# A hybrid encoder block on one core: another bank for a few columns, sixteen blocks in the first selection, splits two ahead, and a last norm per tile

## The chip, the cores and the metric

The kernel runs on one core of a Trainium2 chip. Its metric is the device time of one execution in microseconds (us), the median of several runs. Five engines work side by side and meet only at semaphores: PE (TensorE, matmuls), DVE (VectorE), ACT (ScalarE), POOL (GpSimd) and SP (SyncE, which here only issues DMAs). All tensors come from and go to HBM.

## The reference

512 tokens and 16 meta tokens of width 1024 pass one layer. Cut to what matters here:

```python
h = layer_norm(concat([meta, x]))                       # embed
y = hybrid_mixer(h)        # retention (4 heads) and gated DeltaNet (8 heads), merged, times w_out
h = layer_norm(ALPHA * h + y)
q = (h @ w_q).reshape(L, 8, 2, 128)                      # expert retrieval, 8 heads
s = einsum('lhpd,hpnd->lhpn', q, sub_keys)               # 128 keys on each of two sides
# top 16 of each side, top 16 of the 256 sums -> 16 of 128 * 128 experts per head and token
y = sum over the 8 * 16 chosen of  gelu(h . u[expert]) * gate * v[expert]
out = layer_norm(ALPHA * h + y)[:, 16:]                  # ALPHA = 2 ** 0.25
```

## The kernel before, in words

All large matmuls take float32 operands split in two bfloat16 halves, high and low, and multiply three pairs of halves (`pair_matmul`, L149). ACT makes the high half (a copy), POOL the low half (value minus high half). Both are queued per 128x1024 slice, and PE waits for the low one.

**Retention** (0 to about 460 us) loops over 4 heads. Per head PE projects q, k, v and a gate, scores, outputs, and turns the normalised rows (`turn_rows`, L480). Every product has a PSUM bank in the list `order`; `wait_free` before a product waits until the bank's last reader is done. The 16 meta columns of the keys (`km`) are produced together with k0 and k1, so the wait for their bank stands in front of k0 (bank 2). In a head k0 follows right behind the turned rows y0 to y3 (banks 3 to 6) of the head before it, whose last readers are the low halves that DVE makes (L625). k1 is in bank 3.

**Retrieval** (`retrieve`, about 1415 to 1840 us). The 512 tokens are four tiles. DVE runs the top-k selection of a tile (`tile`), a serial chain of about 80 us. Beside it PE works through the first expert layer for the 384 tokens of tiles 0 to 2 (`Hidden`), in 128 blocks of 128 experts: per block n, SP loads 512 KB of u; ACT splits it (`split_hi`, L1805), POOL makes the low half (`split_lo`, L1821), PE runs 24 matmuls (`form`, L149 with 384 columns), ACT applies gelu (`apply_gelu`, L1813) and SP stores the result. `us` has two slots, so the split of block n+2 waits until block n is formed. `SHARES` says how many blocks run beside each tile's selection: 12, 20, 20, 20. ACT's Exp of the selection stands four blocks before the end of a share and waits for DVE. At the end of a share PE turns the chosen columns, ACT copies them (`picked`, L2025), and PE computes the next tile's scores (L1977).

For the last tile (128 tokens, the first that is selected) the dot products are done row by row instead: POOL gathers u rows for one of the 128 picks k (`gather`, L1874, 512 KB each, by indirect DMA), DVE multiplies and sums them with the tile's rows (`dot`, L1883). A gather waits until the dot that last used its slot is done (4 slots, in `spread` 6).

**Spread** (`spread`, about 1840 to 2160 us) does the other 56 blocks. In the first 48, the busy ones, it also scatters the gates of 4 tokens at a time into dense 128x128 grids: DVE makes one-hot tiles (L2234, L2238), ACT scaled low parts (`low_halves`, L2277), PE 16 small matmuls per block (L2264) behind the block's `form`, ACT copies the result (L2288), and stores 512 KB chunks during four of the six spans of 8 blocks. DVE does 3 dots per two blocks, each in front of the next one-hot tile. The order on ACT per block is split of n+1, gelu of n, two copies, eight low parts; on POOL it is low half of n, then one or two gathers. The last 8 blocks are plain (form, gelu, split). 8 dots are left for them. SP stores blocks 124 to 127 and loads the first four blocks of the next stage; behind the store of block 124 it waits for all 128 dots, since the value slots served as gather slots. The other three stores are queued behind that wait.

**Experts** (`experts`, about 2160 to 2703 us) is the second layer: per block 18 matmuls (L2443) that accumulate in banks 0 to 5 from the first block (`start=first`) to the last; DVE multiplies the gates in (L2487, L2490), makes the low half of the product (L2492), and adds one gathered row of v to the last tile's sum, which is in banks 6 and 7 (`own`, L2497). At the end DVE adds ALPHA times h (L2507).

**Finish** (`finish`, about 2704 us to the end) normalises all four tiles in step: statistics on DVE (L2558), Sqrt on ACT, shift and scale on ACT (L2543), gain on DVE (L2571), bias on POOL (L2550), and the stores.

Each stage is a `Block`; all engines meet at its end.

## Time and profile before

| what | value |
|---|---|
| median of 3 runs | 2732.01 us (2730.4 to 2733.27) |
| profiled execution, its own time | 2730.7 us |
| its span, first to last instruction | 2728.9 us |
| mean granted TensorE clock | 0.968 of full speed |
| busy: PE, DVE, ACT, POOL | 2471.7, 1637.2, 998.7, 1214.1 us |
| last matmul begins | 2701.94 us |
| first and last part of the finish | 2704.71 to 2728.9 us |

Start times are microseconds from the span's start. "Idle before" an instruction is how long its engine had nothing to run, with what ended that wait. The granted clock is the share of 2.4 GHz that TensorE was allowed.

### The profile page before, as it was taken

The numbers are of one execution on the slowest core, as the hardware profiler recorded it, in microseconds if no ns is written. First come the engines' busy times: TensorE is split into PE (matmuls) and PEld (weight loads), VectorE is DVE, ScalarE is ACT, GpSimd is POOL, SyncE is SP. The second block draws the span as 40 slices with busy tenths as digits, with TensorE's granted clock in tenths as the row PEclk, the third lists the DMA queues.
The fourth block names the chain that finished last, engine by engine and source line by source line (L and its number), as shares of the span: only waits on it lengthen the run. The fifth ranks groups of instructions, "written<-read, shape, count | busy, mean of one in ns | idle before, by whom it ended". The sixth has DMA issues, their size and how long they took to land. (4 is left out here: it accounts for less than half of the span.)

```text
span 2728.9 us, 43142 instructions
## 1 busy us (share of the span) xinstructions
PE 2471.7 (91%) x14285; PEld 1389.3 (51%) x14285; DVE 1637.2 (60%) x3379; ACT 998.7 (37%) x1740; POOL 1214.1 (44%) x744
## 2 busy tenths in 40 slices
PE   5999998987999999988979899987888899999995
PEld 3444443444777777775434555555555444444442
DVE  5023132026777777763340878888888477777877
ACT  4212212213333333332312333337888333333332
POOL 4312303313121222211513466666666677777775
PEclk9999998998999999989989999999999999999998
DMA  5302202120000100001322387777998899999995
GB/s 186 100 20 72 88 5 93 62 81 32 31 23 31 31 31 31 8 0 62 108 74 96 117 271 246 244 255 251 375 340 327 266 330 327 329 329 328 329 327 197
DMA packets 174309, 440.24 MB, mean 161 GB/s; under 512 B 17409, under 2 KB 83585, under 8 KB 174097
## 3 DMA queue, kind: packets, MB, share of 16 engines
q1 hardware_dynamic: 132752, 288.20, 30.6%
q0 software_dynamic: 36864, 134.23, 14.8%
q10 hardware_dynamic: 4608, 16.78, 1.6%
q8 instruction: 41, 0.67, 0.1%
q14 instruction: 44, 0.35, 0.0%
HBM read 395.11 MB, written 44.04 MB: 161 GB/s over the span
## 5 line engine op out<-in xcount | busy, mean ns | idle before, releaser
L149 PE MATMUL bank<-hT_hi,hid_u_hi 128*128 128x384 bf16 x1024 | 337.0, 329 | 67.2 <-POOL hid_u_lo L1821 41.2
L1821 POOL TENSOR_TENSOR hid_u_lo<-hid_u,hid_u_hi 128x1024 bf16<-128x1024 f32 x128 | 291.6, 2278 | 213.1 <-ACT hid_u_hi L1805 212.5
L149 PE MATMUL bank<-hT_lo,hid_u_hi 128*128 128x384 bf16 x1024 | 336.9, 329 | 0.0
L149 PE MATMUL bank<-hT_hi,hid_u_lo 128*128 128x384 bf16 x1024 | 336.5, 329 | 0.0
L204 POOL TENSOR_TENSOR ret_w_lo<-ret_w_raw,ret_w_hi 128x1024 bf16<-128x1024 f32 x72 | 153.3, 2162 | 393.6 <-ACT ret_w_hi L199 393.6
L2477 POOL TENSOR_TENSOR ex_v_lo<-ex_v,ex_v_hi 128x1024 bf16<-128x1024 f32 x128 | 272.3, 2127 | 121.0 <-ACT ex_v_hi L2460 120.9
L2443 PE MATMUL bank<-ex_v_hi,ex_gated_hi 128*128 128x512 bf16 x768 | 291.4, 379 | 27.7 <-DVE ex_gated_lo L2492 9.4
L2443 PE MATMUL bank<-ex_v_hi,ex_gated_lo 128*128 128x512 bf16 x768 | 291.6, 380 | 0.0
L2443 PE MATMUL bank<-ex_v_lo,ex_gated_hi 128*128 128x512 bf16 x768 | 291.6, 380 | 0.0
L2463 ACT ACTIVATE ex_gated_hi<-ex_gated 128x384 bf16<-128x384 f32 x128 | 66.9, 523 | 349.5 <-DVE ex_gated L2490 311.4
L2497 DVE SCALAR_TENSOR_TENSOR wide<-ex_row,row_gated,wide 128x1024 f32<-128x1024 f32 x128 | 164.9, 1288 | 49.0 <-DMA ex_row<-in_peer_v,row_index 47.3
L149 PEld LDWEIGHTS bank<-hT_hi,hid_u_hi 128*128 128x128 bf16 x1024 | 100.6, 98 | 154.3 <-issue 86.8
L1319 POOL TENSOR_TENSOR dn_q_decayed<-dn_exp_b,dn_q_k 128x512 f32<-128x512 f32 x16 | 19.9, 1266 | 323.1 <-DVE dn_q_k L1356 323.1
L2487 DVE TENSOR_TENSOR ex_gated<-ex_gated,ex_weights 128x256 f32<-128x256 f32 x128 | 163.2, 1275 | 0.0
L1813 ACT ACTIVATE hid_gelu<-bank 128x384 f32<-128x384 f32 x128 | 62.7, 490 | 258.3 <-PE bank L149 254.4
L2443 PEld LDWEIGHTS bank<-ex_v_hi,ex_gated_hi 128*128 128x128 bf16 x768 | 74.8, 97 | 161.6 <-issue 43.5
L2472 POOL DMA_INDIRECT ex_row<-in_peer_v,row_index x128 | 123.2, 963 | 28.5 <-DVE wide L2501 9.8
L149 PEld LDWEIGHTS bank<-hT_hi,hid_u_lo 128*128 128x128 bf16 x1024 | 100.9, 99 | 68.0 <-issue 2.4
L2460 ACT ACTIVATE ex_v_hi<-ex_v 128x1024 bf16<-128x1024 f32 x128 | 133.2, 1041 | 3.4 <-PEq L2189 3.4
L1805 ACT ACTIVATE hid_u_hi<-hid_u 128x1024 bf16<-128x1024 f32 x128 | 134.2, 1048 | 0.2 <-ACT ex_grid L2288 0.2
L149 PEld LDWEIGHTS bank<-hT_lo,hid_u_hi 128*128 128x128 bf16 x1024 | 100.8, 98 | 60.1 <-issue 2.2
L204 POOL TENSOR_TENSOR dn_w_lo<-dn_w_raw,dn_w_hi 128x1024 bf16<-128x1024 f32 x36 | 78.7, 2198 | 107.6 <-ACT dn_w_hi L199 107.6
(485 smaller groups left out, 5720.3 us busy)
## 6 DMA issues: line engine op xcount, KB each, us to landing
hid_u<-in_peer_u SPq DMA_DIRECT2D x128, 512.0 KB
ex_v<-in_peer_v SPq DMA_DIRECT2D x128, 512.0 KB, 5.4
ret_w_raw<-in_w_ret SPq DMA_DIRECT2D x60, 512.0 KB, 4.3
expert_hidden<-hid_gelu SPq DMA_DIRECT2D x128, 192.0 KB
ex_gated<-expert_hidden SPq DMA_DIRECT2D x128, 192.0 KB
dn_w_raw<-in_w_dn SPq DMA_DIRECT2D x36, 512.0 KB, 3.6
expert_weights<-ex_grid ACTq DMA_DIRECT2D x32, 512.0 KB
ex_weights<-expert_weights SPq DMA_DIRECT2D x64, 256.0 KB
```

Source lines behind the costliest of these rows:

```text
L149: last = nc.tensor.matmul(out, left[l], right[r], start=start and i == 0, stop=stop and i == len(PASSES) - 1)
L204: self.nc.gpsimd.tensor_tensor(self.pairs[slot][1][:, m % 4, :, :], self.raw[:, m % self.RING, :, :], self.pairs[slot][0][:, m % 4, :, :], ...
L1805: self.nc.scalar.activation(self.us[0][:, m % 2, :, :], self.u32[:, m % RING, :, :], ACT.Copy).then_inc(self.u_hi, 1)
L1813: self.nc.scalar.activation(self.act_out[:, m % RING, :], self.core.banks[4 + m % 2][:, 0:DENSE], ACT.Gelu).then_inc(self.gelu, 1)
L1821: self.nc.gpsimd.tensor_tensor(self.us[1][:, m % 2, :, :], self.u32[:, m % RING, :, :], self.us[0][:, m % 2, :, :], ALU.subtract).then_inc ...
L2443: last = nc.tensor.matmul(core.banks[u][:, :], gs[l][:, slot, t * P:(t + 1) * P], vs[r][:, slot, half * 512:(half + 1) * 512], start=first ...
L2460: nc.scalar.activation(vs[0][:, m % SLOTS, :], v32[:, m % RING, :], ACT.Copy)\
L2463: nc.scalar.activation(gs[0][:, m % SLOTS, :], g32[:, m % RING, :], ACT.Copy)\
L2472: nc.gpsimd.indirect_dma_start(row[:, n % RING, :], None, rows_dram[:, :], bass.IndirectOffsetOnAxis(ap=incoming.index[:, n:n + 1], axis=0))\
L2477: nc.gpsimd.tensor_tensor(vs[1][:, n % SLOTS, :], v32[:, n % RING, :], vs[0][:, n % SLOTS, :], ALU.subtract).then_inc(s["v_lo"], 1)
L2487: nc.vector.tensor_tensor(out_part, out_part, wt[:, m % RING // 2, :, m % 2, :], ALU.mult)
L2497: nc.vector.scalar_tensor_tensor(out=own[:, :], in0=row[:, m % RING, :], scalar=incoming.row_gated[:, cols], in1=own[:, :], op0=ALU.mult, ...
```

## The change

Four edits. (1) `km` goes to bank 7 and `v2` to bank 4. (2) The first share has 16 blocks, so retrieval does 76 and the spread stage 52, with 4 plain ones. (3) ACT splits block n+2 right behind gelu of block n; POOL's low halves are one more block ahead, so blocks 76 and 77 are split before and at the start of the spread stage; in the spread stage a block's gathers are queued in front of the low half of n+2. (4) PE starts the sums of the last stage with ALPHA times h (a float32 matmul with a scaled identity), DVE normalises straight from PSUM, tile by tile, the gathered tile first, with gain and bias folded into two operations; `finish` is gone as a stage, ACT only takes the roots and POOL has no part.

```diff
@@ -377,8 +377,8 @@
         act_steps, dve_steps, logit_ready, strip_arg, strip_ready, q_ready, k_ready, var_ready, std_ready, y_ready = (
             core.sem("ret_" + n) for n in ("act_steps", "dve_steps", "logit_ready", "strip_arg", "strip_ready",
                                            "q_ready", "k_ready", "var_ready", "std_ready", "y_ready"))
-        order = ([("q0", 0), ("q1", 1), ("k0", 2), ("k1", 3), ("km", 4)]
-                 + [("v0", 5), ("v1", 6), ("v2", 7), ("v3", 0), ("v4", 1)]
+        order = ([("q0", 0), ("q1", 1), ("k0", 2), ("k1", 3), ("km", 7)]
+                 + [("v0", 5), ("v1", 6), ("v2", 4), ("v3", 0), ("v4", 1)]
                  + [("g0", 2), ("g1", 3), ("g2", 4), ("g3", 5)]
                  + [("s0", 6), ("s1", 7), ("s2", 0), ("s3", 1), ("s4", 2)]
                  + [("o0", 3), ("o1", 4), ("o2", 5), ("o3", 6)]
@@ -1722,7 +1722,7 @@
 RING = 4
 DENSE = SEQ - P
 TILES = (NT - 1,) + tuple(range(NT - 1))
-SHARES = (12, 20, 20, 20)
+SHARES = (16, 20, 20, 20)
 PICKS = PH * TOPK
 BESIDE_TILE = 16
 BESIDE_TURN = 3
@@ -2002,11 +2002,12 @@
                             g = 4 * (n + weights.blocks) + c
                             weights.hi(act, g, g, n % weights.blocks)
                 hidden.split_hi(act, 0, 0)
+                hidden.split_hi(act, 1, 1)
                 gathered.hold_x(act)
                 def step(n, m):
-                    hidden.split_hi(act, n + 1, m + 1)
                     hidden.apply_gelu(act, n, m)
+                    hidden.split_hi(act, n + 2, m + 2)
                 for t in range(NT):
                     for c in range(4):
@@ -2039,6 +2040,7 @@
                                 k < min((s - 1) * BESIDE_TILE + j + 1 + AHEAD, (NT - 1) * BESIDE_TILE):
                             gathered.gather(pool, k)
                             k += 1
+                hidden.split_lo(pool, blocks, blocks)
             @block.vector
             def _(dve):
@@ -2280,8 +2282,8 @@
                 def step(n, m, side, turn, in_span, u0):
-                    hidden.split_hi(act, n + 1, m + 1)
                     hidden.apply_gelu(act, n, m)
+                    hidden.split_hi(act, n + 2, m + 2)
                     for u in range(u0, u0 + per):
                         bk.wait_full(act, f"w{u}", turn)
                         token = in_span * TURN + u * G
@@ -2328,9 +2330,9 @@
                     span_steps(spans - 2 + side, side, False, side == 0)
                 def plain(n, m):
-                    if n < BLOCKS - 1:
-                        hidden.split_hi(act, n + 1, m + 1)
                     hidden.apply_gelu(act, n, m)
+                    if n < BLOCKS - 2:
+                        hidden.split_hi(act, n + 2, m + 2)
                 for n in range(blocks + busy, BLOCKS):
                     plain(n, RING + n % RING)
@@ -2338,15 +2340,20 @@
             @block.gpsimd
             def _(pool):
+                hidden.split_lo(pool, blocks + 1, blocks + 1)
                 for k in range(dots_before, dots_before + RING):
                     gathered.gather(pool, k, dots_before)
                 k = dots_before + RING
                 for n in range(blocks, BLOCKS):
-                    hidden.split_lo(pool, n, n)
                     for _ in range((1, 2)[n % 2] if n < blocks + busy else 1):
                         if k < PICKS:
                             gathered.gather(pool, k, dots_before)
                             k += 1
+                    if n + 2 < BLOCKS:
+                        hidden.split_lo(pool, n + 2, n + 2)
+                while k < PICKS:
+                    gathered.gather(pool, k, dots_before)
+                    k += 1
                 assert k == PICKS
@@ -2386,11 +2393,12 @@
             .then_inc(self.arrived["weights"][slot], 16)
-def experts(core, incoming, acc):
+def experts(core, incoming, a, acc, out, ident):
...
-        names = "v_hi v_lo gated gated_hi gated_lo used row_added summed".split()
+        gain = sbuf(nc, ctx, "fin_gain", [P, D])
+        bias = sbuf(nc, ctx, "fin_bias", [P, D])
+        stats = sbuf(nc, ctx, "fin_stats", [P, NT, 12])
+        mv = sbuf(nc, ctx, "fin_mv", [P, NT, 2])
+        rstd = sbuf(nc, ctx, "fin_rstd", [P, NT])
+        scaled_ident = sbuf(nc, ctx, "ex_scaled_ident", [P, P])
+        names = ("v_hi v_lo gated gated_hi gated_lo used row_added summed ident_ready gb_in fin_steps var_ready std_ready "
+                 "row_ready stored").split()
         s = {n: core.sem("ex_" + n) for n in names}
...
                 over_blocks(sp, RING, BLOCKS, load)
+                sp.dma_start(gain[:, :], a["ln2_g"].partition_broadcast(P)).then_inc(s["gb_in"], 16)
+                sp.dma_start(bias[:, :], a["ln2_b"].partition_broadcast(P)).then_inc(s["gb_in"], 16)
+                for turn, tile in enumerate(ORDER):
+                    sp.wait_ge(s["row_ready"], turn + 1)
+                    sp.dma_start(out[tile * P:(tile + 1) * P, :], acc[:, tile, :]).then_inc(s["stored"], 16)
+                sp.wait_ge(s["stored"], 16 * NT)
...
-                                                    start=first and i == 0, stop=last_one and i == 2)
+                                                    start=False, stop=last_one and i == 2)
...
+                pe.wait_ge(s["ident_ready"], 1)
+                for u, (half, t) in enumerate(UNITS):
+                    nc.tensor.matmul(core.banks[u][:, :], scaled_ident[:, :], acc[:, t, half * 512:(half + 1) * 512],
+                                     start=True, stop=False)
...
+                for turn in range(NT):
+                    act.wait_ge(s["var_ready"], turn + 1)
+                    nc.scalar.activation(rstd[:, turn:turn + 1], mv[:, turn, 1:2], ACT.Sqrt)\
+                        .then_inc(s["std_ready"], 1)
...
+                nc.vector.tensor_scalar(scaled_ident[:, :], ident[:, :], ALPHA, None, ALU.mult)\
+                    .then_inc(s["ident_ready"], 1)
-                for u, (half, t) in enumerate(UNITS):
-                    dve.wait_ge(s["summed"], u + 1)
-                    part = acc[:, t, half * 512:(half + 1) * 512]
-                    nc.vector.scalar_tensor_tensor(out=part, in0=part, scalar=ALPHA, in1=core.banks[u][:, :],
-                                                   op0=ALU.mult, op1=ALU.add)
-                nc.vector.tensor_copy(acc[:, NT - 1, :], own[:, :]).then_inc(s["row_added"], 1)
-                dve.wait_ge(s["row_added"], BLOCKS + RING + 1)
...
-def finish(core, a, acc, out):
...
-                nc.scalar.activation(rstd[:, :], mv[:, :, 1], ACT.Sqrt).then_inc(std_ready, 1)
-                    nc.scalar.activation(acc[:, t, :], acc[:, t, :], ACT.Identity, bias=shift[:, t:t + 1],
-                                         scale=rstd[:, t:t + 1]).then_inc(normed, 1)
-                    nc.gpsimd.tensor_tensor(acc[:, t, :], acc[:, t, :], bias[:, :], ALU.add)\
-                link(nc.vector.reciprocal(rstd[:, :], rstd[:, :]))
-                link(nc.vector.tensor_tensor(shift[:, :], mv[:, :, 0], rstd[:, :], ALU.mult))
-                nc.vector.tensor_scalar(shift[:, :], shift[:, :], -1.0, None, ALU.mult).then_inc(shift_ready, 1)
-                    nc.vector.tensor_tensor(acc[:, t, :], acc[:, t, :], gain[:, :], ALU.mult).then_inc(gained, 1)
+                def halves(tile):
+                    if tile == NT - 1:
+                        return [own[:, half * 512:(half + 1) * 512] for half in range(2)]
+                    return [core.banks[2 * tile + half][:, :] for half in range(2)]
+                def moments(turn, tile):
+                    for half, row_half in enumerate(halves(tile)):
+                        if turn:
+                            dve.wait_ge(s["summed"], 2 * tile + half + 1)
+                        ins = nc.vector.bn_stats(stats[:, turn, 6 * half:6 * half + 6], row_half)
+                    link(ins)
+                    link(nc.vector.bn_aggr(mv[:, turn, :], stats[:, turn, :]))
+                    nc.vector.tensor_scalar(mv[:, turn, 1:2], mv[:, turn, 1:2], LN_EPS, None, ALU.add)\
+                        .then_inc(s["var_ready"], 1)
+                def normalise(turn, tile):
+                    dve.wait_ge(s["std_ready"], turn + 1)
+                    link(nc.vector.reciprocal(rstd[:, turn:turn + 1], rstd[:, turn:turn + 1]))
+                    for half, row_half in enumerate(halves(tile)):
+                        cols = slice(half * 512, (half + 1) * 512)
+                        ins = nc.vector.scalar_tensor_tensor(out=acc[:, tile, cols], in0=row_half,
+                                                             scalar=mv[:, turn, 0:1], in1=gain[:, cols],
+                                                             op0=ALU.subtract, op1=ALU.mult)
+                    link(ins)
+                    nc.vector.scalar_tensor_tensor(out=acc[:, tile, :], in0=acc[:, tile, :],
+                                                   scalar=rstd[:, turn:turn + 1], in1=bias[:, :],
+                                                   op0=ALU.mult, op1=ALU.add).then_inc(s["row_ready"], 1)
+                dve.wait_ge(s["gb_in"], 32)
+                for turn, tile in enumerate(ORDER):
+                    moments(turn, tile)
+                    if turn:
+                        normalise(turn - 1, ORDER[turn - 1])
+                normalise(NT - 1, ORDER[NT - 1])
...
-            experts(core, incoming, h0)
-        finish(core, a, h0, out)
+            experts(core, incoming, a, h0, out, ident)
```

## Rows read from the trace of the kernel before

**Rows 1.** Who PE waited for, 0 to 620 us: total us, times, longest.
```profile
PE bank L149 <- DVE ret_yT_lo L625: 12.2, 3, 4.1
```
**Rows 2.** Timeline at the first change of heads: start, length, engine, idle before.
```profile
154.41 0.39 PE L149 MATMUL bank<-hT_hi,ret_w_hi 128*128 128x512 bf16 x1 [4.02 <-DVE ret_yT_lo L625]
```
**Rows 3.** Stretches: length, busy PE, PEld, DVE, ACT, POOL, granted clock, DMA share, GB/s.
```profile
155.25:158.60 3.35, 3.35 (x17) 1.27 (x14) 0.30 (x1) 0.00 (x0) 0.00 (x0) 0.51 0.00 0
259.25:264.80 5.55, 5.55 (x25) 2.20 (x26) 1.14 (x2) 0.00 (x0) 0.00 (x0) 0.52 0.00 0
...
1554.20:1558.40 4.20, 4.20 (x14) 2.02 (x15) 4.17 (x2) 0.00 (x0) 3.87 (x1) 0.53 0.47 145
...
1584.95:1589.15 4.20, 4.20 (x16) 2.11 (x17) 4.20 (x18) 0.00 (x0) 2.88 (x2) 0.59 1.01 383
```
**Rows 4.** Timeline of the retrieval: PE's waits at the shares' ends and starts.
```profile
1554.17 0.50 PE L149 MATMUL bank<-hT_hi,hid_u_hi 128*128 128x384 bf16 x1 [6.71 <-POOL hid_u_lo L1821]
...
1584.94 0.32 PE L149 MATMUL bank<-hT_hi,hid_u_hi 128*128 128x384 bf16 x1 [2.94 <-issue]
...
1644.90 0.34 PE L149 MATMUL bank<-hT_hi,hid_u_hi 128*128 128x384 bf16 x1 [1.34 <-POOL hid_u_lo L1821]
```
**Rows 5.** Timeline from retrieval into the spread stage: PE's first block, ACT's third gelu.
```profile
1848.12 0.50 PE L149 MATMUL bank<-hT_hi,hid_u_hi 128*128 128x384 bf16 x1 [10.28 <-POOL hid_u_lo L1821]
...
1867.64 0.49 ACT L1813 ACTIVATE hid_gelu<-bank 128x384 f32<-128x384 f32 x1 [3.54 <-PE bank L149]
```
**Rows 6.** Who PE waited for in the spread stage, 1860 to 2125 us.
```profile
PE bank L149 <- POOL hid_u_lo L1821: 17.1, 12, 1.7
PE bank L149 <- issue: 16.6, 14, 2.2
```
**Rows 7.** Timeline: one gather of u rows and the dot that uses it.
```profile
1959.21 0.96 POOL L1874 DMA_INDIRECT ex_v<-in_peer_u_rows,row_index  x1
...
1968.90 1.22 DVE L1883 CUSTOM_DVE_ANT_0 ex_gated<-ex_v,wide 128x1024 f32<-128x1024 f32 x1 [2.65 <-DMA ex_v<-in_peer_u_rows,row_index]
```
**Rows 8.** DMA of eight busy blocks (1906 to 1951 us), and a half of them by stretch.
```profile
DMA packets 5165, 16.21 MB, mean 360 GB/s; under 512 B 570, under 2 KB 1594, under 8 KB 5164
...
1906.25:1928.75 22.50, 19.77 (x161) 12.99 (x160) 18.44 (x36) 19.13 (x49) 14.41 (x10) 1.00 1.02 408
```
**Rows 9.** Timeline from the last busy block (its gelu) to the experts' first matmul.
```profile
2121.94 0.49 ACT L1813 ACTIVATE hid_gelu<-bank 128x384 f32<-128x384 f32 x1 [0.29 <-PE bank L149]
...
2135.89 0.95 POOL L1874 DMA_INDIRECT ex_v<-in_peer_u_rows,row_index  x1
...
2141.25 1.22 DVE L1883 CUSTOM_DVE_ANT_0 ex_weights<-ex_v,wide 128x1024 f32<-128x1024 f32 x1 [2.13 <-DMA ex_v<-in_peer_u_rows,row_index]
...
2155.77 0.49 ACT L1813 ACTIVATE hid_gelu<-bank 128x384 f32<-128x384 f32 x1 [3.41 <-PE bank L149]
...
2159.89 1.23 DVE L2501 TENSOR_SCALAR wide<-h 128x1024 f32<-128x1024 f32 x1 [3.04 <-PEq L2189]
...
2165.15 0.58 PE L2443 MATMUL bank<-ex_v_hi,ex_gated_hi 128*128 128x512 bf16 x1 [9.41 <-DVE ex_gated_lo L2492]
```
**Rows 10.** A float32 product of 512 columns (two records each), and 100 us of experts.
```profile
429.37 5.42 PE L460 MATMUL bank<-ret_q,ret_k 128*128 128x512 f32 x12
...
2200.00:2300.00 100.00, 96.44 (x431) 40.27 (x430) 78.86 (x96) 35.27 (x48) 73.51 (x48) 1.00 0.96 327
```
**Rows 11.** Timeline: the same kind of norm at 1372 us, and the end of the kernel.
```profile
1371.27 0.69 DVE L1696 SCALAR_TENSOR_TENSOR h<-h,bank 128x512 f32<-128x512 f32 x1 [4.49 <-PE bank L149]
1372.00 1.29 DVE L1701 BATCH_NORM_STATS2 mix_stats<-h 128x6 f32<-128x512 f32 x2
...
1375.03 1.23 DVE L1711 TENSOR_TENSOR h<-h,mix_gain 128x1024 f32<-128x1024 f32 x1
...
2698.09 1.28 DVE L2497 SCALAR_TENSOR_TENSOR wide<-ex_row,row_gated,wide 128x1024 f32<-128x1024 f32 x1
...
2713.75 12.11 POOL L2550 TENSOR_TENSOR h<-h,fin_bias 128x1024 f32<-128x1024 f32 x4 [17.21 <-DVE h L2571]
```

49 lines of the change are left out of this document (3 added, 46 removed).

## The prediction

> **What bounds the kernel now.** I read the share of busy time first (PE is busy for 91% of the span), then who PE waited for, stage by stage, then the timeline around each wait. PE sets the end almost everywhere, so a part of the change is worth the PE idle time that it takes away in front of a matmul, plus what the clock costs afterwards. The reader is to see four places. (a) In the retention stage PE stands three times for about 4 us at a change of heads, 12.2 us in all [rows 1, 2]. (b) In retrieval it stands at the end of the first share, at the start of the second, and once near the end of each later share [rows 4]. (c) At the boundary it waits 10.28 us for one low half [rows 5], and in the busy blocks about 1.3 us in every second block, again for low halves [rows 6]. (d) Around the last stage it waits 9.41 us before the first matmul [rows 9], and from 2702 us on it has nothing to do. Behind the long idles the granted clock is about half (1.2 instead of 2.4 GHz): 0.51 for 3.35 us after the first change of heads, 0.52 for 5.55 us after the second and likewise after the third, 0.53 for 4.20 us after 6.71 us idle, 0.59 for 4.20 us after 2.94 us idle [rows 3]. The many idles of 1.0 to 1.5 us left the clock alone. The time lost at such a clock is length times what is missing to 1.
>
> **1. `km` in bank 7.** k0's matmuls wait for y1's low half only because `km` shares y1's bank. In bank 7 the last reader is long done. k0 itself needs bank 2, read long ago. k1 needs y0's low half, which DVE makes before y1's, so before 154.41; k0 started without its wait would run to about 156.3. `v2` comes 25 us later still. So nothing takes the wait's place: -12.2 us [rows 1], and the slow clock behind it goes too: 3.35 x 0.49 + 2 x 5.55 x 0.48 = 7.0 [rows 3]. Sum **-19.2**; the bound from below is 12.2, if the clock falls all the same.
>
> **2. Sixteen blocks first, and the new order in retrieval.** With 12 blocks ACT stands at the Exp behind block 7 while block 9's split is queued behind it, and PE idles 6.71 us [rows 4]. With 16, ACT gets there four blocks (15.7 us) later, when DVE has been ready for some 8 us: the wait goes, with 4.20 x 0.47 = 2.0 of clock [rows 3]. The new order differs from the old one only where something stands between a split and a gelu. At a share's end block e+1 is split before `picked` is copied, so its low half no longer waits for the scores' copies, and the four gathers of the second share no longer stand in front of the low half that PE needs: -2.94 - 4.20 x 0.41 = -4.7 [rows 3, 4]. Before the Exp the split of block e-3 comes first: 3 x 1.34 = -4.0 [rows 4]. Against it, that same early split (1.05 us, ACT's split in the profile's groups) now stands in front of `picked`, and PE's scores wait for it: 3 x 1.05 = +3.2, and about +0.4 behind the first Exp. Four more blocks cost 4 x 3.93 = +15.7 here (24 matmuls at 0.163 us) and go out of the tail (point 4). Sum: retrieval ends -8.7 - 4.7 - 4.0 + 3.6 + 15.7 = **+1.9** us later. DVE's selection has about 3 us of slack against PE in the later tiles, which falls to about 1.8 here; if it were the bound, 3 us of gain would go.
>
> **3. Boundary and busy blocks.** Block 76 has both halves when the stage starts, so PE starts about 3.3 us after the last block of retrieval (1.05 more than the engines need now, for the same split) instead of 10.6. But the block's grid needs its second one-hot tile; that stands behind a dot, the dot behind its gather (5.3 us), and the gather now behind the low half of block 77 (2.13). I count about 14.5 us from the last block to the grid and 25.7 to the third gelu, with a slow clock left in block 77. Now it is 30.1: retrieval's last block ends at about 1837.5 (1848.12 - 10.28, less the transposes), the third gelu starts at 1867.64 [rows 5]. So **-4.4**, bounds 0 and -8.
>
> From there to the last busy gelu (2121.94) [rows 9] are 45 blocks in 254.3 us, 11.3 per two blocks. PE's idle in them is about 30 us, the 33.7 of that view without its ends [rows 6], so -30 is the lower bound: 9.95 per two blocks. In the new order the high half is made right behind gelu, 3.4 us (two copies, eight low parts) sooner, so the low half is never late by itself. ACT needs 4.8 us per block, PE 5.0. What is late next? The gathers. Gather(n) stood behind low half n; now it stands behind low half n+1, some 3 us later against PE. The one that is late is the third dot of each pair. Counted from the end of a block's form: split and low half +4.0, gather to dot 8 to 10 us in the loaded stretches (9.69 with DVE waiting for the DMA) [rows 7], dot and one-hot tile +1.6, ACT's low part +1.3: 14.9 to 16.9 against 15.6 when PE wants it. So 0 to 1.3 us stay in a pair where chunks are stored (two thirds of the blocks), and about nothing in the others. I take 10.75 and 10.25: 15 x 0.5 + 7.5 x 1.05 = **-15.4**, bounds 0 and -30.
>
> The DMA bears it: these blocks move 16.21 MB per eight, and half of such a span ran at 408 GB/s [rows 8]. At that rate eight blocks need 39.7 us, 9.9 per pair, just under PE's own need. By the Trainium skill (DMA: Bandwidth & Descriptors, "Specifications") HBM gives a core some 358 GB/s; by that the storing spans could not become shorter at all. The 408 of the trace does not agree with it as a limit here, and the measurement decides.
>
> **4. The tail.** Count from the last busy form's end, T. Now the experts' stage starts at 2159.89 = T + 38.0 [rows 9]. Four plain blocks fewer make that T + 22.3. But the last dots have less time. Gather 127 was issued at 2135.89, four blocks before the last form, and its dot began 5.4 us later [rows 9]; SP's wait behind the store of block 124 cost nothing. Now gathers 124 to 127 run one per plain block: the low half of 127 ends at about T + 12.8, gathers 126 and 127 follow at 12.9 and 14.2, the dot ends at T + 20.9. Only then SP issues the loads of four blocks and the stores of 125 to 127, which need 5.3 us of issuing; the last store lands 3.5 us later: T + 30 instead of T + 21. So the edit is worth 30.2 - 38.0 = **-7.8**, not -17. Bounds: -15 (dots never late) and -5 (3.3 MB of loads at 408 GB/s in front of the last store).
>
> **5. Start of the experts.** The six float32 products are 12 records of 0.43 us [rows 10], 5.1 us, or 7.2 with the clock still low in the first 4 us. PE waits 5.3 us there anyway (2159.89 to 2165.15), and its first ten matmuls ran slow. The stage goes at 100 / (431 / 18) = 4.18 us per block where 18 matmuls need 3.9 [rows 10], so PE catches up what it starts late. DVE, which sets that pace, gets one small operation more: **+0.2**, bounds 0 and +3.
>
> **6. The last norm.** DVE is free at 2699.3 behind the last row [rows 11]. Statistics of a tile: 1.29 + 0.21 + 0.15 and semaphores = 1.74; normalising: a reciprocal 0.2, two halves from PSUM 2 x 0.69, one pass of 1.23 = 2.8 [rows 11]. Four tiles: 18.2, and 0.3 for the last root: 2717.8. The roots lie beside the next tile's statistics. The last store now ends 3.0 us after POOL's last add (2713.75 + 12.11 = 2725.86) [rows 11]: 2720.8 instead of 2728.9, **-8.1**. The end of PE (2702.3) is in no tile's way. Bounds -10 and -5.
>
> **Sum.** -19.2 + 1.9 - 4.4 - 15.4 - 7.8 + 0.2 - 8.1 = -52.8. The profiled execution took 2730.7 (its span is 2728.9), which gives 2677.9; the median of the runs shown is 1.3 higher: 2679.2. I say **2679**; own range 2664 to 2694.
>
> **The rivals.** *Late gathers hold the busy blocks* (0.18): the loop from gather to dot to one-hot tile to grid becomes the pace, since each gather now starts 3 us later and waits for a dot six back. For it: DVE already waits for gathers' DMA [rows 7]. Against it: only one dot in three is tight. The 15.4 would shrink to about 3: 2691. *DMA is the bound in the storing spans* (0.07): transfers of several queues together stop at about the 360 GB/s that eight blocks average now [rows 8], so no gain in 30 of the blocks, 7.5 less: 2687. It is what the Trainium skill's page on DMA bandwidth, cited above, would give. *The clock gives nothing back* (0.06): 7.0 in retention and 3.7 in retrieval stay lost: 2690; the rows of many short idles without a fall speak against it. *The tail is not late* (0.06): dots keep up, 2671. *The other side* (0.02): in front of the low halves the gathers block POOL itself. A gather whose slot is not free holds the low half of n+2, that holds PE, PE holds the grid and the next dots. It decides where two blocks cost 11.3 + (52.8 - 15.4) / 22.5 = 13.0 us or more; then 2732 and above. Against it: the gather has six slots, and 1.2 us between issues is enough. My forecast has 0.61.
>
> **Numbers.** 0.2% is 5.5 us, about what a measurement can tell from no change. All cases but the last are faster by more: faster 0.97, same 0.01, slower 0.02. The range takes in the late gathers with a cheap clock above, and PE without idle below: 2662 to 2699.
>
> **What would show it.** Right: no PE idle behind L625 and a full clock at the changes of heads; `picked` 1.05 us later; no idle at the first Exp; two busy blocks at 10.2 to 10.8; PE idle for some 14 us in front of the float32 products, with SP's stores of 125 to 127 behind the last dot; DVE's two scalar-tensor-tensor forms per tile, ending about 18.5 us after the last row. Wrong: DVE waits for gathers of more than 1 us in most pairs, low halves behind a blocked gather, or the selection ending after PE's blocks.

## The result

The changed kernel takes 2692.89 us (median of 4 runs, 2690.18 to 2694.08) where the kernel before took 2731.39 (4 runs, 2730.4 to 2733.27): a ratio of 0.9856, 95% interval 0.9841 to 0.9872. The forecast was 2679, its own range 2664 to 2694, the whole range 2662 to 2699. The change does what it says, and the gain is 14 us smaller than worked out. The profiled execution took 2690.18, its span is 2688.4.

The table sets each point of the forecast beside the two profiled executions. A stage begins and ends at the same instruction in both: first product of retrieval (L1977), last gelu of retrieval's last block, third gelu behind it, gelu of the last busy block (T; block 123, before the change 119), first instruction of VectorE in the last stage, end of the last row's L2526, end of the span.

| point | forecast | measured | before, us | after, us |
|---|---|---|---|---|
| 1 retention and all ahead of retrieval | -19.2 | -18.8 | 1506.9 | 1488.1 |
| 2 retrieval | +1.9 | +5.6 | 330.6 | 336.3 |
| 3 boundary | -4.4 | -4.5 | 30.1 | 25.6 |
| 3 busy blocks (45) | -15.4 | -12.0 | 254.3 | 242.3 |
| 4 tail | -7.8 | -5.3 | 38.0 | 32.7 |
| 5 last stage up to the last row | +0.2 | +3.0 | 539.5 | 542.4 |
| 6 last norm | -8.1 | -8.5 | 29.5 | 21.0 |
| sum | -52.8 | -40.5 | 2728.9 | 2688.4 |

**The changes of heads** ran as forecast: nobody waits for L625 any more, and the clock is full in the stretches around all three, where it was half behind each wait [rows 1 to 3]. Windows of the changed kernel, columns as in [rows 3]:

```profile
150.00:156.00 6.00, 6.00 (x51) 3.52 (x49) 5.65 (x10) 2.06 (x4) 0.00 (x0) 1.00 0.00 0
250.00:262.00 12.00, 12.00 (x101) 6.10 (x99) 5.31 (x9) 1.11 (x3) 0.00 (x0) 1.00 0.00 0
355.00:367.00 12.00, 12.00 (x80) 5.74 (x77) 4.82 (x12) 0.60 (x1) 0.00 (x0) 1.00 0.00 0
```

**Retrieval.** The 6.71 and 2.94 us idles of [rows 4] are gone. Those of 1.34 us are not: 1.29, 1.26 and 1.25 us of them are left. Timeline of the changed kernel, PE:

```profile
1559.79 0.38 PE L1977 MATMUL bank<-ex_grid 128*128 128x128 f32 x1 [1.58 <-ACT picked L2026]
...
1629.70 0.33 PE L149 MATMUL bank<-hT_hi,hid_u_hi 128*128 128x384 bf16 x1 [1.29 <-POOL hid_u_lo L1821]
```

The second row answers to the third of [rows 4]; its like stand at 1718.60 and 1807.49 (1.26 and 1.25 us). The first shows the price of a split in front of `picked`, paid three times. The low half that PE waits for is itself long. POOL and DVE around it:

```profile
1622.07 2.12 POOL L1821 TENSOR_TENSOR hid_u_lo<-hid_u,hid_u_hi 128x1024 bf16<-128x1024 f32 x1 [0.62 <-ACT hid_u_hi L1805]
...
1626.06 3.40 POOL L1821 TENSOR_TENSOR hid_u_lo<-hid_u,hid_u_hi 128x1024 bf16<-128x1024 f32 x1 [0.76 <-ACT hid_u_hi L1805]
1629.96 3.64 POOL L1821 TENSOR_TENSOR hid_u_lo<-hid_u,hid_u_hi 128x1024 bf16<-128x1024 f32 x1 [0.50 <-ACT hid_u_hi L1805]
```
```profile
1625.19 2.29 DVE L2109 TENSOR_TENSOR ex_grid<-top_rank_f,top_iota 128x2048 f32<-128x2048 f32 x1
1627.51 4.09 DVE L2112 TENSOR_TENSOR ex_grid<-ex_grid,top_best_index_f 128x2048 f32<-128x2048 f32 x1
```

The times fit together as turns. DVE's first operation ends at 1627.48, and POOL's, begun at 1626.06, ends 1.98 us later, at 1629.46. DVE's second begins at 1627.51, lasts 4.09 us (it takes 2.29 where no low half is running when it starts, see share12) and ends 2.14 us after that low half, at 1631.60. The next low half ends 2.00 us after that. That fits an engine that waits until the other is done and then needs about 2 us; by itself the low half takes 2.13. At the other two shares' ends the distances are the same within 0.01 us. ScalarE's Exp begins only at 1631.19 (its table load at 1629.90), when PE has already waited.

A second wait of this kind stands in the middle of a share, beside another operation of the selection (L2093). It took 0.95, 1.02 and 1.06 us before the change and takes 1.25, 1.61 and 1.55 now (at the first of them it is the gather in front of the low half that is long, 3.03 us where 0.95 is usual). The low half and PE behind it, at the second of the three (timeline of the changed kernel):

```profile
1681.02 2.27 DVE L2093 TENSOR_TENSOR ex_grid<-top_best 128x2048 f32<-128x2048 f32 x1
1681.57 3.72 POOL L1821 TENSOR_TENSOR hid_u_lo<-hid_u,hid_u_hi 128x1024 bf16<-128x1024 f32 x1 [0.75 <-ACT hid_u_hi L1805]
...
1685.53 0.33 PE L149 MATMUL bank<-hT_hi,hid_u_hi 128*128 128x384 bf16 x1 [1.61 <-ACT hid_u_hi L1805]
```

The view names ScalarE here, since its next split happened to end last; PE starts 0.24 us behind the end of the low half (1685.29), as it does at 1629.70.

**The busy blocks.** From one gelu to the next it is 5.13 us in the steady blocks. In each of the four storing spans some three blocks take 5.7 to 6.8. They are not the first four, behind which the chunks are issued, but begin three or four blocks behind the first of those. In the first storing span (blocks 84 to 91) the steps behind 84, 85 and 86 take 5.15 us each, those behind 87 to 90 take 6.77, 5.97, 6.26 and 4.78 (23.8 us for the four), and the next four 20.6 again, although the next chunks are already being issued in three of them. Windows of the changed kernel, one block each, the second, fourth and fifth of that span:

```profile
1885.30:1890.50 5.20, 4.96 (x41) 3.25 (x40) 5.20 (x8) 4.80 (x13) 4.08 (x3) 1.00 0.95 301
...
1895.70:1902.50 6.80, 5.31 (x40) 3.16 (x40) 6.70 (x12) 4.74 (x14) 3.93 (x3) 1.00 1.03 416
1902.50:1908.40 5.90, 4.96 (x40) 3.22 (x40) 4.66 (x7) 4.77 (x13) 3.22 (x4) 1.00 1.03 420
```

The queues' totals over the four slow blocks (1895.7 to 1919.5) and the four that follow:

```profile
DMA packets 3081, 9.58 MB, mean 402 GB/s; under 512 B 357, under 2 KB 976, under 8 KB 3080
```
```profile
DMA packets 2114, 6.73 MB, mean 327 GB/s; under 512 B 217, under 2 KB 622, under 8 KB 2114
```

And who waited in the stage, with total, times and longest:

```profile
ACT hid_u_hi L1805 <- DMA hid_u<-in_peer_u: 14.4, 12, 2.1
ACT spread_first_lo L2279 <- DVE spread_place L2236: 12.4, 34, 0.4
PE bank L2266 <- ACT spread_first_lo L2279: 9.0, 31, 0.9
...
DVE ex_gated L1883 <- DMA ex_v<-in_peer_u_rows,row_index: 5.2, 4, 2.0
```

The low halves of [rows 6] no longer appear; PE now waits for ACT's low parts, and ACT for loads of u that land late, 12 times, three per storing span.

**The tail.** Timeline from the last dot to the last stage's first bf16 product:

```profile
2112.60 0.33 SPq L2385 DMA_DIRECT2D ex_gated<-expert_hidden  x1
...
2118.19 0.48 SPq L1783 DMA_DIRECT2D expert_hidden<-hid_gelu  x1
...
2124.91 0.23 DVE L2530 TENSOR_SCALAR ex_scaled_ident<-ident 128x128 f32<-128x128 f32 x1 [11.39 <-PEq L2191]
2125.20 1.22 PE L2474 MATMUL bank<-h,ex_scaled_ident 128*128 128x512 f32 x1 [16.30 <-DVE ex_scaled_ident L2530]
...
2132.76 0.38 PE L2464 MATMUL bank<-ex_v_hi,ex_gated_hi 128*128 128x512 bf16 x1
```

SyncE issues from 2112.60 on, as the forecast had it, and the last store at T + 26.0 (forecast 26.2). The stage starts 6.7 us behind that store, not 3.5. The idle in front of the float32 products is 16.3 us (forecast 14).

**The end.** Timeline: a wait before the second last row, the first statistics, the last pass, the stores.

```profile
2658.99 1.29 DVE L2526 SCALAR_TENSOR_TENSOR wide<-ex_row,row_gated,wide 128x1024 f32<-128x1024 f32 x1 [4.20 <-DMA ex_row<-in_peer_v,row_index]
...
2667.38 1.29 DVE L2547 BATCH_NORM_STATS2 fin_stats<-wide 128x6 f32<-128x512 f32 x2
...
2684.07 1.28 DVE L2562 SCALAR_TENSOR_TENSOR h<-h,fin_rstd,fin_bias 128x1024 f32<-128x1024 f32 x1
```

From the last row to the last pass DVE needs 18.0 us (forecast 18.5), and the last store ends 3.0 later (forecast 3.0). The 4.20 us in front is new; before, the last four rows waited 0.22 us in all.

### The profile page after: what moved, and what is told of

It reads as the page before. It is cut to its first block and busy times, and to the rows that moved or that the text cites. A ratio compares the mean times of both kernels' runs of the same rounds, so it can differ in the third digit from the quotient of the medians.

```text
span 2688.4 us, 43155 instructions
## 1 busy us (share of the span) xinstructions
PE 2469.1 (92%) x14297; PEld 1388.9 (52%) x14297; DVE 1662.2 (62%) x3385; ACT 992.6 (37%) x1739; POOL 1206.7 (45%) x740
## 5 line engine op out<-in xcount | busy, mean ns | idle before, releaser
L2464 PE MATMUL bank<-ex_v_hi,ex_gated_hi 128*128 128x512 bf16 x768 | 291.2, 379 | 20.6 <-ACT ex_gated_hi L2488 3.1
L2526 DVE SCALAR_TENSOR_TENSOR wide<-ex_row,row_gated,wide 128x1024 f32<-128x1024 f32 x128 | 164.7, 1286 | 45.4 <-DMA ex_row<-in_peer_v,row_index 44.2
L2516 DVE TENSOR_TENSOR ex_gated<-ex_gated,ex_weights 128x256 f32<-128x256 f32 x128 | 171.0, 1336 | 0.0
L1805 ACT ACTIVATE hid_u_hi<-hid_u 128x1024 bf16<-128x1024 f32 x128 | 134.1, 1048 | 14.4 <-DMA hid_u<-in_peer_u 14.4
L2279 ACT ACTIVATE spread_first_lo<-spread_place,spread_weight_low 128x128 bf16<-128x128 bf16 x384 | 121.0, 394 | 23.1 <-DVE spread_place L2236 23.1
```

The lines of the kernel that those rows point to most:

```text
L1805: self.nc.scalar.activation(self.us[0][:, m % 2, :, :], self.u32[:, m % RING, :, :], ACT.Copy).then_inc(self.u_hi, 1)
L2279: ins = nc.scalar.activation(first[1][:, u, i, :], place[:, u, i, :], ACT.Copy, scale=weight_low[:, tokens(u * G + i)])
L2464: last = nc.tensor.matmul(core.banks[u][:, :], gs[l][:, slot, t * P:(t + 1) * P], vs[r][:, slot, half * 512:(half + 1) * 512], start=False ...
L2516: nc.vector.tensor_tensor(out_part, out_part, wt[:, m % RING // 2, :, m % 2, :], ALU.mult)
L2526: nc.vector.scalar_tensor_tensor(out=own[:, :], in0=row[:, m % RING, :], scalar=incoming.row_gated[:, cols], in1=own[:, :], op0=ALU.mult, ...
```

## Experiments

Times of different chips are compared by their ratio to the kernel before, run on the same chip. The first product of retrieval comes between 1486.3 and 1492.5 us in kernels that are alike up to there, so a difference of a few us between two medians says little, and the stages say more. Their lengths in the profiled executions, us; retrieval counts here from its first gelu (7.7 us behind the first product):

| kernel | ratio, 95% | retrieval | boundary | busy | tail | last stage | norm |
|---|---|---|---|---|---|---|---|
| changed | 0.9856 (0.9841 to 0.9872) | 328.5 | 25.6 | 242.3 | 32.7 | 542.4 | 21.0 |
| km_back | 0.9931 (0.9914 to 0.9947) | 328.4 | 26.2 | 243.9 | 33.3 | 543.5 | 21.0 |
| picked_first | 0.9864 (0.9848 to 0.9881) | 326.1 | 26.6 | 242.1 | 32.9 | 541.8 | 21.1 |
| no_rank | 0.9841 (0.9825 to 0.9858) | 321.1 | 26.5 | 243.2 | 32.7 | 542.4 | 21.0 |
| gb_early | 0.9870 (0.9853 to 0.9886) | 328.3 | 26.2 | 243.1 | 32.6 | 539.4 | 21.1 |
| tail_stores | 0.9837 (0.9821 to 0.9853) | 328.6 | 26.4 | 243.2 | 27.7 | 544.3 | 21.0 |
| even_stores | 0.9813 (0.9798 to 0.9828) | 329.6 | 26.3 | 232.0 | 33.0 | 542.4 | 21.1 |
| small_stores | 0.9815 (0.9799 to 0.9832) | 329.6 | 26.2 | 231.0 | 32.7 | 541.6 | 21.0 |
| quarter_low | 0.9829 (0.9808 to 0.9850) | 328.5 | 25.6 | 237.8 | 31.3 | 543.2 | 21.0 |
| share12 | 0.9844 (0.9831 to 0.9858) | 319.2 | 26.4 | 243.4 | 37.2 | 543.0 | 21.5 |
| gathers_behind | 1.0007 (0.9998 to 1.0016) | 329.4 | 26.3 | 280.5 | 35.5 | 541.8 | 21.1 |
| behind_six | 0.9854 (0.9838 to 0.9869) | 329.2 | 26.0 | 242.9 | 31.3 | 541.5 | 21.0 |
| best | 0.9811 (0.9797 to 0.9824) | 315.6 | 26.1 | 232.1 | 40.0 | 542.4 | 21.0 |

Stages that an edit doesn't touch repeat within about 2 us, the boundary and the norm within 1.

**km_back: point 1 alone.**

```diff
-        order = ([("q0", 0), ("q1", 1), ("k0", 2), ("k1", 3), ("km", 7)]
-                 + [("v0", 5), ("v1", 6), ("v2", 4), ("v3", 0), ("v4", 1)]
+        order = ([("q0", 0), ("q1", 1), ("k0", 2), ("k1", 3), ("km", 4)]
+                 + [("v0", 5), ("v1", 6), ("v2", 7), ("v3", 0), ("v4", 1)]
```

> The changed kernel with point 1 undone: km in bank 4 and v2 in bank 7 again, all else as changed. The theory (PE waits at three changes of heads only for y1's bank, and the clock falls behind each wait) expects all of the 18.8 us that the first matmul of retrieval came earlier to go back: about 2711.5, with three idles of about 4 us in front of L625's matmuls and a clock near half for 3 to 6 us behind them. Rival (part of the 18.8 us came from elsewhere, or the clock would have risen anyway): about 12 us or less go back, 2705 or below.

Measured: 2710.7, and retrieval's first product at 1506.52. The waits are back (who PE waited for, 0 to 620 us):

```profile
PE bank L149 <- DVE ret_yT_lo L625: 12.5, 3, 4.5
```

12.5 us of idle explain two thirds of the 18.4 us. Behind the three waits the granted clock is 0.58 over 3.3 us and 0.53 and 0.55 over 5.3 us each, as in [rows 3], which loses 3.3 x 0.42 + 5.3 x 0.47 + 5.3 x 0.45 = 6.3 us; the two together are 18.8. The bank alone is worth nearly half of the whole gain.

**picked_first.** Each share's last `split_hi` moves behind the copy:

```diff
-                    over_blocks(act, ends[t + 1] - RING, ends[t + 1], step)
+                    for n in range(ends[t + 1] - RING, ends[t + 1] - 1):
+                        step(n, RING + n % RING)
+                    hidden.apply_gelu(act, ends[t + 1] - 1, RING + (ends[t + 1] - 1) % RING)
                     bk.wait_full(act, "t", t)
...
+                    hidden.split_hi(act, ends[t + 1] + 1, RING + (ends[t + 1] + 1) % RING)
```

> The changed kernel, but at the end of a share ScalarE copies picked (L2026) before it splits the block after next, instead of behind that split. Theory (each of the three later share ends pays 1.0 us because picked stands behind a split of 1.05 us, and PE's scores wait for picked): 3 us less, 2690, PE's wait for picked back at about 0.6 us; the delayed split costs nothing because its block is wanted 7 us later. Rival (the low half of that block, which starts 0.6 us later, is then late for PE): no gain, with the idle in front of a matmul that reads hid_u_lo in its place.

Measured: PE waits 0.63 us for `picked` instead of 1.58, three times, and retrieval is 2.4 us shorter (expected 3). The delayed low half costs 0.4 us once (a wait of 1.93 us where the changed kernel has 1.55). So the mechanism holds; the median, 2691.7, is too coarse to show it.

**no_rank.** It leaves out part of the selection, the translation of ranks to keys:

```diff
                     for side in range(2):
-                        link(nc.vector.tensor_tensor(
-                            left[:, :, :, :], rankf[:, side, :, :].unsqueeze(3).broadcast_to(wide),
-                            iota[:, :].unsqueeze(1).unsqueeze(1).broadcast_to(wide), ALU.is_equal))
-                        link(nc.vector.tensor_tensor(
-                            left[:, :, :, :], left[:, :, :, :],
-                            of_rank[:, :, side, :].unsqueeze(2).broadcast_to(wide), ALU.mult))
-                        nc.vector.tensor_reduce(chosen[:, 1 + side, :, :], left[:, :, :, :], AX.X, ALU.add)\
+                        nc.vector.tensor_copy(chosen[:, 1 + side, :, :], of_rank[:, :, side, :])\
                             .then_inc(chosen_ready, 1)
```

> The changed kernel, but the selection leaves out the translation of ranks to key numbers: per side two tensor-tensor operations over 2048 elements and a reduction (L2109 to L2115) become one copy of 128 elements, so the chosen keys are other ones (still valid). ScalarE's Exp stays where it is. Theory (the idle of 1.25 to 1.29 us in front of one block near the end of each share comes from GpSimd's low half, which takes 3.4 us instead of 2.13 beside VectorE's tensor-tensor operations): all low halves there take about 2.1 us, the three idles go, about 4 us less in retrieval: 2689. Rival (the Exp with its two table loads on ScalarE, as my recorded step has it): the idles stay at 1.2 us or more, 2693.

Measured: all three idles are gone (3.8 us), and so are the 0.43 us ones two blocks later (1.3) and two of the first share (0.48 and 0.57); retrieval is 7.4 us shorter, so that about 1 us of it shows in no such wait. The waits in mid-share, beside L2093, which this kernel keeps, are still there (1.06, 1.60 and 1.61 us). POOL in the same place as above (timeline):

```profile
1624.49 2.13 POOL L1821 TENSOR_TENSOR hid_u_lo<-hid_u,hid_u_hi 128x1024 bf16<-128x1024 f32 x1 [0.76 <-ACT hid_u_hi L1805]
1628.39 2.12 POOL L1821 TENSOR_TENSOR hid_u_lo<-hid_u,hid_u_hi 128x1024 bf16<-128x1024 f32 x1 [1.77 <-ACT hid_u_hi L1805]
```

The Exp is still there, at 1629.63 with both its table loads, and PE doesn't stop. So the 1.3 us come from DVE's and POOL's turns, not from the Exp.

**gb_early.** `gain` and `bias` are loaded ahead of `over_blocks(sp, RING, BLOCKS, load)` instead of behind it.

> The changed kernel, but SyncE issues the loads of gain and bias (512 KB each) at the start of the last stage, in front of block 4's loads, instead of behind block 127's. Theory (the two transfers compete with the last row gathers, and VectorE's wait of 4.2 us for the second last row is most of the 3.0 us that the experts took longer): the wait near the end goes, 3 to 4 us less: 2689.5. Rival (the wait comes from something else, or the same bytes delay the first blocks as much): within 1 us of 2693.

Measured: the last stage takes 539.4 us, the same as before the change (539.5), and none of the last six rows is waited for. That is the whole 3.0. The median, 2691.68, doesn't show it.

**tail_stores.**

```diff
                 for n in range(BLOCKS - RING, BLOCKS):
                     hidden.store(sp, n, n)
+                for n in range(BLOCKS - RING, BLOCKS):
                     if n == BLOCKS - RING:
                         sp.wait_ge(gathered.dotted, PICKS + RING)
```

> The changed kernel, but SyncE stores the hidden blocks 124 to 127 before it waits for the last dots, and only the loads for the last stage come behind that wait. Theory (the stage ends late because three stores stand behind that wait and behind 3.3 MB of loads; the last of them lands 6.7 us after it is issued): the last stage starts about 6 us sooner; the float32 products then cover the loads' landing, so 5 to 6 us less: 2687.5. Rival (the last stage waits for its loads instead, which are issued at the same moment as now): the stage starts sooner, but its first bf16 matmul comes only 0 to 2 us sooner: 2691 or more.

Measured: the tail is 5.0 us shorter and the last stage 1.8 longer, 3.2 us together, which lies between the two forecasts. Against T the stage starts 5.0 us sooner, and so does its first bf16 product, but its first row comes only 3.3 us sooner: DVE waits 2.47 us for it where it waited 0.71.

```profile
2132.76 1.29 DVE L2527 SCALAR_TENSOR_TENSOR wide<-ex_row,row_gated,wide 128x1024 f32<-128x1024 f32 x1 [2.47 <-DMA ex_row<-in_peer_v,row_index]
```

**even_stores and small_stores: bytes in the busy blocks.** The first spreads the same stores; the second stores an eighth of the bytes.

```diff
-                        if j < span_blocks // 2 and stores:
-                            for chunk in range(2 * j, 2 * j + 2):
+                        if stores:
+                            for chunk in ((0, 1), (2,), (3,), (4,), (5,), (6,), (7,), ())[j]:
                                 store(1 - side, t - 1, chunk)
```
```diff
-                    keys = slice(NK // CHUNKS * chunk, NK // CHUNKS * (chunk + 1))
+                    keys = slice(NK // CHUNKS * chunk, NK // CHUNKS * chunk + 2)
...
-        two = slice(n, n + 2) if isinstance(n, int) else bass.ds(n, 2)
+        two = slice(0, 2)
```

> The changed kernel, but the eight chunks of a span's grid are stored by the first seven blocks of the next span (2, 1, 1, 1, 1, 1, 1) instead of by its first four (2, 2, 2, 2). Theory (the busy blocks of 6.0 us and more are those four: they move 2.5 MB each, and 417 GB/s is all that the transfers reach; the average over eight blocks would fit): the slow blocks go, busy blocks take 5.2 us nearly throughout, 8 to 11 us less: 2683.5. Rival 1 (they are slow because VectorE's one-hot tiles and GpSimd's low halves slow each other down): no change, 2693. Rival 2 (the last chunk, issued near the end of the span, lands late, and ScalarE waits for it before it writes the next span): four waits of 2 us or more, no gain.

> The changed kernel, but each chunk stores 2 keys instead of 16, and the last stage loads the first two keys' weights for every block (so its output has wrong weights outside one half of a die's work); all counts of instructions and waits stay. Theory (bytes moved set the pace of the storing blocks): all busy blocks at 5.15 us, 45 in 232 us, 10 us less in that stage, no window over 350 GB/s. Rival (VectorE and GpSimd contending): the busy blocks stay at 242 us.

Measured: 232.0 and 231.0 us of busy stage, 10.3 and 11.3 less. One span of even_stores (windows), and the transfers of small_stores over its stage:

```profile
1931.00:1972.00 41.00, 39.65 (x322) 25.96 (x320) 40.37 (x74) 38.15 (x98) 29.25 (x21) 1.00 1.02 397
```
```profile
DMA packets 27220, 69.73 MB, mean 302 GB/s; under 512 B 3023, under 2 KB 12879, under 8 KB 27212
```

Eight blocks in 41 us, and PE busy for 39.65 of them. Spreading the stores gets nearly all that leaving most of their bytes out would. ScalarE never waits for a span's last chunk, and for loads of u it waits twice, 2.0 us in all, instead of 12 times and 14.4. This one edit takes the kernel to 2683.35.

**quarter_low.** `split_lo` works on `0:KC // 4` in the stage of busy blocks; the other three quarters keep old values.

> The changed kernel, but in the stage of busy blocks GpSimd makes only the first quarter of each low half (the rest keeps what stood there, so the hidden layer is computed a little less exactly). Theory (a one-hot tile on VectorE takes longer while a low half runs on GpSimd): the mean of VectorE's three one-hot forms falls towards its shortest, by 0.1 to 0.3 us, and the steady blocks go from 5.13 to the 5.0 that PE needs; the storing blocks, bound by bytes, stay at 6 us. So 3 to 5 us less: 2689. Rival (contention sets the storing blocks too): 10 us less or more.

Measured: 237.8 us, 4.5 less. The first one-hot form (groups, DVE) in the changed kernel and in this one:

```profile
L2236 DVE TENSOR_TENSOR spread_place<-spread_numbers,spread_keys_of 128x512 bf16<-128x512 bf16 x89 | 87.7, 986 | 3.2 <-issue 1.9 <-DVE row_dots L1891 1.3
```
```profile
L2236 DVE TENSOR_TENSOR spread_place<-spread_numbers,spread_keys_of 128x512 bf16<-128x512 bf16 x89 | 39.5, 444 | 10.1 <-PE bank L2266 7.5 <-DVE row_dots L1891 2.5
```

The tile needs 0.44 us beside quarter low halves and 0.99 beside full ones, 48 us of DVE time in the stage; only 4.5 us reach the end. They come from the spans without stores, where a block takes 4.79 us instead of 5.13 (I had expected 5.0). A storing span of eight blocks takes 43.8 us in the mean against 44.0: there a faster DVE gains nothing.

**share12.** `SHARES = (12, 20, 20, 20)`, so 16 in the first share is undone.

> The changed kernel with 12 blocks in the first share again, so four blocks go from retrieval to the plain blocks of the tail. The four blocks take 15.7 us out of retrieval. Against that, the stall at the first Exp comes back, but I expect only part of the 6.71 us and 2.0 us of slow clock that it cost before the change: in the new order the block e-3 is split before ScalarE gets to the Exp, which gives PE one block (3.9 us) more to work on, and the low half after it comes 0.5 us later. So 3.3 us idle and 1.7 us of slow clock, less the 1.0 us of small idles that stand there now: retrieval 11.7 us shorter. In the tail eight plain blocks cover the last dots, so it takes 38.0 us as before the change instead of 32.7. Theory (each edit's worth depends on the other: the late dots eat what 16 blocks gain): 6 us less, 2686.5. Rival (the stall at the Exp comes back whole, as my recorded sum has it): retrieval 7 us shorter and 2 us less in all, 2691. Rival 2 (16 blocks pay, as the recorded sum has it): 2693 or more.

Measured: retrieval 9.3 us shorter and the tail 4.5 longer. The stall at the first Exp is 5.01 us (expected 3.3, before 6.71). PE's row, and DVE's and POOL's ahead of it (timeline):

```profile
1537.98 0.48 PE L149 MATMUL bank<-hT_hi,hid_u_hi 128*128 128x384 bf16 x1 [5.01 <-POOL hid_u_lo L1821]
```
```profile
1533.60 2.29 DVE L2112 TENSOR_TENSOR ex_grid<-ex_grid,top_best_index_f 128x2048 f32<-128x2048 f32 x1
```
```profile
1534.54 3.34 POOL L1821 TENSOR_TENSOR hid_u_lo<-hid_u,hid_u_hi 128x1024 bf16<-128x1024 f32 x1 [5.94 <-ACT hid_u_hi L1805]
```

Of the missing 1.7 us, 1.2 are again a turn: the low half begins at 1534.54, DVE's operation ends at 1535.89, and the low half 1.99 us after that, where it needs 2.13 by itself. DVE's operation, which had no low half in front of it, took its 2.29 us.

The two stages that the edit touches give 4.8 us for 12 blocks, but the others took 3.0 us more in this trace; the median (2686.49) agrees in sign, and the two intervals overlap. No gain of sixteen blocks shows; whether they lose is not settled.

**gathers_behind: the order of POOL alone.**

```diff
+                    if n + 2 < BLOCKS:
+                        hidden.split_lo(pool, n + 2, n + 2)
                     for _ in range((1, 2)[n % 2] if n < blocks + busy else 1):
                         ...
-                    if n + 2 < BLOCKS:
-                        hidden.split_lo(pool, n + 2, n + 2)
```

> The changed kernel, but in the stage of busy blocks GpSimd issues its gathers behind the low half of the block after next, instead of in front of it. Theory (bytes moved hold the storing blocks, VectorE and ScalarE hold the others at 5.15 us, and no gather is in time's way): the busy stage stays at 242 us within 2, the tail takes 1 to 2 us more because the last gathers are issued 2 us later: 2694. Rival (the gathers' lateness is what still holds the busy blocks, so another 2 to 3 us makes it worse): VectorE's waits for gathers rise from 10 us to 25 or more, and the stage takes 5 us more or worse: 2699.

Measured: 2731.29, as slow as before the change. My theory for this run is wrong, and the rival was right in kind and much too small: the busy stage takes 38.2 us more. Who DVE waited for there:

```profile
DVE ex_weights L1883 <- DMA row_ring<-in_peer_u_rows,row_index: 30.7, 12, 5.4
DVE ex_gated L1883 <- DMA ex_v<-in_peer_u_rows,row_index: 27.5, 11, 4.2
```

I had also put the delay at 2 to 3 us. It is one place in POOL's order, that is a whole block: the gathers of block n now stand behind low half n + 2, which can't be made until block n is through PE and ScalarE.

**behind_six.** The same order, with the first gathers issued six ahead:

```diff
-                for k in range(dots_before, dots_before + RING):
+                for k in range(dots_before, dots_before + ring):
...
-                k = dots_before + RING
+                k = dots_before + ring
```

> The kernel of the run gathers_behind (gathers behind the low halves), but GpSimd issues six gathers instead of four when the stage of busy blocks begins, so that every later gather is issued two dots (1.33 blocks, 7 us) ahead of where it was. Theory (that run lost 38 us because each gather is issued about 2 to 3 us too late and closes a loop: gather, dot, one-hot tile, low part, grid product, the next block's form, gelu, split, low half, gather; a lead of two dots takes more than that out): the stage of busy blocks comes back from 280 us to 242 or less, VectorE waits for gathers less than 10 us in all, and the kernel takes 2693. Rival (a gather behind a low half is slow or blocks GpSimd for another reason, for instance because its slot is not free): most of the 38 us stays, 2715 or more.

Measured: 2689.82, the busy stage at 242.9 us. The waits of DVE for gathers there:

```profile
DVE ex_gated L1883 <- DMA row_ring<-in_peer_u_rows,row_index: 0.3, 1, 0.3
```

All 38 us come back, so it was lateness. And the reverse: with gathers waited for 0.3 us in all instead of 9.5, the stage is no shorter than the changed kernel's 242.3. Gathers hold nothing in the changed kernel; they have just enough lead.

**best.** even_stores, gb_early, picked_first, share12 and tail_stores in one kernel.

> The changed kernel with five edits of the runs before, put together: chunks stored 2, 1, 1, 1, 1, 1, 1 (10.3 us of the busy stage), gain and bias loaded at the start of the last stage (3.0 us of it), picked copied in front of the split at a share's end (2 us), 12 blocks in the first share (4.7 us over retrieval and tail), and the hidden stores of blocks 124 to 127 in front of the wait for the last dots (nothing here, since with eight plain blocks the last dots are early). If the stages' gains add up: 20 us less than the changed kernel, 2673. Rival (some meet each other: loads of gain and bias beside the first row gathers, or the last store still setting the end of the tail): 2678 or more.

Measured: 2678.4. Retrieval and busy stage keep their gains (12.9 and 10.2 us), but the tail takes 40.0 us and the last stage 542.4. SyncE's row says why:

```profile
2095.57 12.01 SPq L1783 DMA_DIRECT2D expert_hidden<-hid_gelu  x4
2107.68 0.38 SPq L2389 DMA_DIRECT2D ex_gated<-expert_hidden  x1
```

With eight plain blocks the last dots are early, and the loads for the last stage were issued between the stores. Now all of them stand behind the last store, and those of gain and bias follow them, 1.3 us ahead of the first row's gather: DVE waits 4.58 us for it. The tail is 2.8 us longer than share12's. tail_stores helps behind 16 blocks and hurts behind 12, so the rival's account of this run is the right one. By ratio best is level with even_stores alone. Without the tail edit it was not tried.

## Why the forecast was right, and 14 us too good

The measured median lies 1.1 us inside the upper end of the own range. The profiled execution is 12.3 us above the sum, and nothing large cancelled: the misses are 3.7 us in point 2, 3.4 in the busy blocks, 2.5 in point 4 and 2.8 in point 5, all to the slow side, and 0.4 or less elsewhere.

**Point 1** held, idle and clock: in km_back 12.5 us of waits and 6.3 of slow clock.

**Point 2** missed by 3.7 us. The step that failed is "Before the Exp the split of block e-3 comes first: 3 x 1.34 = -4.0": the three idles went from 4.0 to 3.8 us. The view says that PE waited for POOL's low half; I put it down to the Exp in front of the split without looking at how long that low half took. It took 3.49 us before the change and 3.40 after, and no_rank shows whose turn it waited for. The waits in mid-share, which the forecast left out, grew by 1.4 us for the same reason, and smaller items took about as much back: the +3.2 for `picked` came as 2.8. The -8.7 at the first Exp came, but it is no gain of sixteen blocks by itself: share12, with twelve and the new order, is no slower.

**Point 3.** The boundary came as written. In the busy blocks the steady pair came (10.3 us against 10.25), and the loaded one was mis-sized: 10.75 forecast, 11.0 measured (44.0 us for the eight blocks of a storing span, in the mean). The sum also has 15 x 0.5 where 11.3 - 10.75 is 0.55, which is 0.7 us. The step that failed is the averaging: "At that rate eight blocks need 39.7 us, 9.9 per pair". The bytes do not come evenly: 9.58 MB moved in the four slow blocks, which at 419 GB/s (the highest that 10 us of the stage showed) is 22.9 us, against 20.6 at the steady pace. even_stores makes the average true and gets 10.3 us. The answer to "What is late next? The gathers" was wrong too, as behind_six shows: it is loads of u behind the stores' bytes, and DVE's one-hot tiles by a little. Nor is 9.95 us per pair PE's own need, as the lower bound had it: quarter_low's steady pairs take 9.6. The rival on DMA (0.07) named the resource, with the wrong limit and for too many blocks. By the Trainium skill (Perfetto Trace Analysis, "Roofline") 358 GB/s is a core's share when both cores of a pair read, and a core alone is held by its 16 DMA engines, in practice at some 120% of that. The 402 GB/s over the four slow blocks and the 419 over 10 us here are 112 and 117% of it and agree.

**Point 4** missed by 2.5. Late dots, SyncE's order and the 5.3 us of issuing came as written; the term mis-sized is "the last store lands 3.5 us later", which was 6.7 with the loads of four blocks beside it (26.2 + 3.5 is 29.7; the sum has 30.2). tail_stores confirms the queue behind the dots.

**Points 5 and 6.** The last norm came within 0.4. The last stage reached its bound of +3, and for a cause that point 5 doesn't count: not the float32 products but two loads of 512 KB, moved by the change from the finish to beside the last rows; gb_early takes them away from there and has the 3.0 us back. The forecast costed what the moved step asks of VectorE and not its transfers.

**The gathers** were the largest risk, and seen from the wrong side. The forecast took the old place, behind the low half, as the safe one and priced the new one at 3 us of lateness. In fact it is two-ahead splits with the old order that would have cost 26 us against before (280.5 to 254.3), and moving the gathers in front avoids that. It is a threshold: a block later costs 38 us, 1.33 blocks earlier again gains nothing.

## What to carry to other kernels

When a stage alternates between loaded and idle stretches, work out bytes per stretch, not per period, and spread the transfers before touching the engines. When a view names an instruction that another engine waits for, read its duration before the queue in front of it: 3.4 us where 2.1 is usual is a cause of its own. When one step of a loop is moved a block ahead, check what else stands behind it on the same engine; a transfer that moves from in front of it to behind it can cost more than the whole change gains.
